# Moving the recurrent unit behind the indexer, and the order of weight chunks that goes with it

## The reference

```python
h = x @ w_in                                    # split among all branches and the gates
# A gated DeltaNet: short causal conv on q, k, v, l2 norm of q and k, chunked rule with a triangular solve
# B sparse attention: rotary, an indexer picks the keys per query (256 of the cache), softmax
# C retention: rotary, multi-scale decay, group norm
# D RG-LRU: conv, then
r  = sigmoid(xb @ w_r + b_r); ig = sigmoid(xb @ w_i + b_i)
a  = exp(-8 * r * softplus(-lam)); b = sqrt(-expm1(2 * log_a)) * (ig * x); h_t = a_t * h_{t-1} + b_t
# E memory cross-attention into 256 memory tokens
ys = each branch * silu(its gate path)
merged = sum(sigmoid(gate_pre[n]) * (ys[n] @ w_branch[n]) for n in range(5))
x = layer_norm(alpha * x + merged @ w_out)
```

## Time and profile before

| | before |
|---|---|
| median of 3 runs | 3231.86 us |
| the profiled execution | 3233.75 us |
| its span, first to last instruction | 3231.9 us |
| PE busy | 2998.8 us, 93% |
| VectorE (DVE) busy | 1702.1 us, 53% |
| ScalarE (ACT) busy | 975.0 us, 30% |
| GpSimd (POOL) busy | 177.1 us, 5% |
| mean granted TensorE clock | 0.947 of full |

### The profile page before, as it was taken

How to read it: one execution, slowest core, us unless ns; L and a number is a source line. 1 busy time by engine, 2 the same in 40 slices (tenths; PEclk the granted TensorE clock), 3 DMA queues, 4 the chain that set the end, 5 groups by cost and what they waited for, 6 DMA issues and landing times. The chain is left out here.

```text
span 3231.9 us, 52427 instructions
## 1 busy us (share of the span) xinstructions
PE 2998.8 (93%) x21612; PEld 2826.4 (87%) x21612; DVE 1702.1 (53%) x2454; ACT 975.0 (30%) x1301; POOL 177.1 (5%) x204
## 2 busy tenths in 40 slices
PE   6998998999999999999789999899999999999995
PEld 5988887998999998999779888789988999989994
DVE  3153367656566756344423533766666657554444
ACT  2232332223253332233313222322233423222232
POOL 0000100000000003100000000000000000030000
PEclk9988998998999999999989889999999999999998
DMA  5565443455656557565256643444655665575661
GB/s 170 163 184 149 144 120 92 115 158 144 175 156 170 148 154 200 166 179 159 70 161 185 194 131 106 127 118 116 168 148 152 168 175 136 161 214 165 167 167 40
DMA packets 830709, 485.98 MB, mean 150 GB/s; under 512 B 26053, under 2 KB 812613, under 8 KB 829219
## 3 DMA queue, kind: packets, MB, share of 16 engines
q1 hardware_dynamic: 809328, 410.00, 47.1%
q0 software_dynamic: 19840, 66.75, 6.6%
q10 hardware_dynamic: 1296, 5.80, 0.5%
HBM read 466.27 MB, written 16.47 MB: 149 GB/s over the span
## 5 line engine op out<-in xcount | busy, mean ns | idle before, releaser
L603 PE MATMUL mb<-xsplit,wsplit 128*128 128x264 f32 (+1 forms) x5312 | 1589.9, 299 | 87.5 <-DVE wsplit L1385 73.8
L604 PE MATMUL mb<-xsplit,wsplit 128*128 128x264 f32 (+1 forms) x5312 | 1538.7, 290 | 0.0
L605 PE MATMUL mb<-xsplit,wsplit 128*128 128x264 f32 (+1 forms) x5312 | 1536.8, 289 | 0.0
L603 PEld LDWEIGHTS mb<-xsplit,wsplit 128*128 128x128 f32 (+1 forms) x5312 | 1031.8, 194 | 124.4 <-issue 54.0
L604 PEld LDWEIGHTS mb<-xsplit,wsplit 128*128 128x128 f32 (+1 forms) x5312 | 1032.2, 194 | 8.0 <-issue 3.8
L605 PEld LDWEIGHTS mb<-xsplit,wsplit 128*128 128x128 f32 (+1 forms) x5312 | 1025.7, 193 | 1.1
L1385 DVE TENSOR_TENSOR wsplit<-ring,wsplit 128x1024 fp32r<-128x1024 f32 (+2 forms) x664 | 776.9, 1210 | 261.3 <-ACT wsplit L1139 247.8
L1139 ACT ACTIVATE wsplit<-ring 128x1024 fp32r<-128x1024 f32 (+2 forms) x664 | 663.3, 1043 | 144.6 <-PE mb L605 104.0
L1166 ACT ACTIVATE gbuf<-mb 128x264 f32<-128x264 f32 x160 | 62.4, 390 | 865.2 <-PE mb L605 852.4
L619 PE MATMUL mb<-work,bring 128*128 128x264 f32 x1280 | 310.6, 385 | 0.0
L1415 DVE TENSOR_TENSOR gbuf<-gbuf,mb 128x264 f32<-128x264 f32 x128 | 54.9, 429 | 456.4 <-PE mb L619 448.8
(11 more groups left out here) (441 smaller groups left out, 2300.6 us busy)
## 6 DMA issues: line engine op xcount, KB each, us to landing
ring<-in_w_in_dram SPq DMA_DIRECT2D x592, 512.0 KB, 4.9
bring<-in_w_branch_dram SPq DMA_DIRECT2D x160, 256.0 KB, 3.1
ring<-in_w_out_dram SPq DMA_DIRECT2D x64, 512.0 KB, 4.5
ring<-in_w_mem_kv_dram SPq DMA_DIRECT2D x32, 512.0 KB, 3.6
work<-in_cache_mem_k_dram POOLq DMA_DIRECT2D x16, 512.0 KB, 4.1
work<-in_cache_mem_v_dram POOLq DMA_DIRECT2D x16, 512.0 KB, 4.2
work<-in_mem_prompt_dram ACTq DMA_DIRECT2D x2, 2048.0 KB, 11.7
work<-in_state_gdn_dram POOLq DMA_DIRECT2D x8, 512.0 KB, 6.6
```

Source lines behind the costliest of these rows:

```text
L603: pe.matmul(bank[0:n, 0:T], wh, ah, start=first, stop=False)
L604: pe.matmul(bank[0:n, 0:T], wh, al, start=False, stop=False)
L605: mm = pe.matmul(bank[0:n, 0:T], wl, ah, start=False, stop=last)
```

## The change

The recurrent unit goes from behind retention to a place directly behind the indexer, on all four engines. Its gate is second in the order of branches (`BRANCH`), and `plan` gives its inputs LX and LZ earlier. The decays, the convolutions, the DeltaNet and retention come behind it, so their steps run beside other chunks: the convolutions beside gate 0, the inverse beside gate 0, RK and gate 1, the DeltaNet's samples beside gate 1, retention beside gate 1, RZ, DK and DV. The norms take 2, 2, 3 and 2 chunks where they took 1, 1, 2 and 3. The unit's results lie in the places of DK, DV and DZ. Its weights are loaded into `tabs` first, by ScalarE at the layer's start as two loads; the levels come after them, by GpSimd, once the second sigmoid is done. Store of RK waits for the unit's last rows, store of RV for the DeltaNet's states, where RZ's store did. 32 chunks are left at the end. In the diff the block of the unit is shown once for each engine where it is added; it is removed unchanged from its old place, apart from indices of waits.

```diff
-PLACE = {GQ: 0, GK: 1, GV: 2, RQ: 3, RK: 4, RV: 5, DQ: 6, DK: 7, DV: 8, DZ: 9, RZ: 10, LZ: 11, IQ: 12, MQ: 13, GZ: 13,
-         MZ: 14, LX: 14}
+PLACE = {GQ: 0, GK: 1, GV: 2, RQ: 3, RK: 4, LX: 4, LZ: 5, DQ: 6, DK: 7, DV: 8, DZ: 9, RZ: 10, RV: 11, IQ: 12, MQ: 13,
+         GZ: 13, MZ: 14}
...
-BRANCH = [(4, MZ), (0, GZ), (2, RZ), (3, LZ), (1, DZ)]
+BRANCH = [(4, MZ), (3, LZ), (0, GZ), (2, RZ), (1, DZ)]
...
-    project(MZ, IQ, DQ, RQ, GQ, GK, GV, GZ, RK, RV)
+    project(MZ, IQ, LX, LZ, RQ, DQ, GQ, GK, GV, GZ)
     gates(0)
-    project(LX, RZ, LZ, DK, DV, DZ)
-    for n in range(1, len(BRANCH)):
-        gates(n)
+    project(RK)
+    gates(1, 0, 12)
+    project(RV)
+    gates(1, 12, KC)
+    project(RZ, DK, DV, DZ)
+    gates(2)
+    gates(3)
+    gates(LAST)
...
-            return H(i_) if i_ < 3 else tmpA
+            return H((DK, DV, DZ)[i_]) if i_ < 3 else tmpA
... PE, behind the indexer
-                    count()
+                    tail(0, LX)
+                    stream(3)
+                    pe.wait_ge(sem.tails_ok, 1)
+                    pe.wait_ge(sem.conv_act, 1)
+                    pe.wait_ge(sem.lw_in, 32)
+                    for i in range(2):
+                        if i:
+                            pe.wait_ge(sem.lru_act, 1)
+                        for h in range(NH):
+                            mm = pe.matmul(bb[:, h, 0:T], lruw[:, i, h, :], H(LX)[:, h, :], start=True, stop=True)
+                        mm.then_inc(sem.lru_mm, 1)
+                        stream(1)
+                    pe.wait_ge(sem.lru_act, 2)
+                    stream(4)
+
+                    pe.wait_ge(sem.lru_o, 1)
+                    for h in range(NH):
+                        mm = pe.transpose(bb[0:NB + 1, 0, h * P:(h + 1) * P], H(LX)[:, h, NP - 1:T], ident)
+                    mm.then_inc(sem.h_mm, 1)
+                    stream(1)
+                    pe.wait_ge(sem.h_rows, 1)
...
                     mm.then_inc(sem.gc_mm, 1)
+                    count()
                     stream(1)
...
-                        stream((1, 1, 2, 3)[n - 1])
+                        stream((2, 2, 3, 2)[n - 1])
...
+                    pe.wait_ge(sem.stored, ready(RV))
... ScalarE
-                                if (x, m) == (RZ, 0):
+                                if (x, m) == (RK, 0):
+                                    act.wait_ge(sem.h_rows, 1)
+                                if (x, m) == (RV, 0):
                                     act.wait_ge(sem.s_out, 16 * NH)
...
-                    act.dma_start(tabs[:, :], a.levels).then_inc(sem.tab_in, 16)
+                    for i, w in enumerate((a.lru_w_r, a.lru_w_i)):
+                        act.dma_start(lruw[:, i, :, :], at_l(w).rearrange("h i j -> i h j")).then_inc(sem.lw_in, 16)
...
+                    stream(1)
+                    ahead()
+                    conv_out(0, LX)
+                    stream(2)
+                    for i in range(2):
+                        ahead()
+                        act.wait_ge(sem.lru_mm, i + 1)
+                        for h in range(CPS):
+                            mm = act.activation(lru(i)[:, h, :], bb[:, h, 0:T], ACT.Sigmoid, bias=qT[:, h, 1 + i:2 + i])
+                        mm.then_inc(sem.lru_act, 1)
+                        stream(1)
+                    for h in range(CPS):
+                        act.activation(lru(2)[:, h, :], lru(0)[:, h, :], ACT.Exp, scale=sn4[:, h:h + 1])
+                        mm = act.activation(lru(3)[:, h, :], lru(0)[:, h, :], ACT.Tanh, scale=sp4[:, h:h + 1])
+                    mm.then_inc(sem.lru_a, 1)
+                    ahead()
+                    stream(1)
+                    ahead()
+                    act.wait_ge(sem.lru_b, 1)
+                    act.activation(lru(0), lru(0), ACT.Sqrt).then_inc(sem.lru_c, 1)
+                    stream(3)
+                    stream(1)
... VectorE
-                            if kind == "gate" and x == LAST and m < 4:
-                                c = slice(4 * m, 4 * m + 4)
+                            if kind == "gate" and x == LAST and 4 <= m < 8:
+                                c = slice(4 * m - 16, 4 * m - 12)
...
+                    conv(0, LX)
+                    stream(2 + 2)
+                    dve.wait_ge(sem.lru_act, 2)
+                    v(dve.tensor_tensor(lru(1), lru(1), H(LX), ALU.mult))
+                    ahead()
+                    dve.wait_ge(sem.lru_a, 1)
+                    ahead()
+                    v(dve.tensor_scalar(lru(0), lru(3), 1.0, None, ALU.add))
+                    v(dve.reciprocal(lru(0), lru(0)))
+                    stream(1)
+                    ahead()
+                    dve.scalar_tensor_tensor(lru(0), lru(3), 2.0, lru(0), ALU.mult, ALU.mult).then_inc(sem.lru_b, 1)
+                    dve.wait_ge(sem.lru_c, 1)
+                    v(dve.tensor_tensor(lru(1), lru(1), lru(0), ALU.mult))
+                    stream(1)
...
                         v(dve.reciprocal(tmpA, tmpA))
                         dve.tensor_tensor(H(s), H(s), tmpA, ALU.mult).then_inc(sem.normed, 1)
-                        stream((1, 1, 2, 3)[n - 1])
+                        stream((2, 2, 3, 2)[n - 1])
...
                     dve.tensor_tensor(H(GZ), H(GZ), H(GQ), ALU.mult).then_inc(sem.normed, 1)
-                    stream(2)
+                    stream(3)
... GpSimd
+                    tail(0, LX)
+                    pool.wait_ge(sem.lru_act, 2)
+                    pool.dma_start(tabs[:, :], a.levels).then_inc(sem.tab_in, 16)
+                    pool.wait_ge(sem.h_rows, 1)
+                    put(o.p_lru[bass.ds(l, 1)].rearrange("z b n -> (z b) n"), stg[0:1, :], sem.lru_out)
+                    put(at_l(o.s_lru), stg[1:NB + 1, :], sem.lru_out)
                     for i, s in enumerate((GQ, GK, GV)):
-                        tail(i, s)
+                        tail(1 + i, s)
```

More of the change, by code:

```diff
@@ L74 @@
 NRING = 4
-BRANCH = [(4, MZ), (0, GZ), (2, RZ), (3, LZ), (1, DZ)]
+BRANCH = [(4, MZ), (3, LZ), (0, GZ), (2, RZ), (1, DZ)]
 LAST = len(BRANCH) - 1
+BRANCH_DONE = [("sy_ok", 1), ("h_rows", 1), ("normed", 3), ("yc_ok", 1), ("sy_ok", 2)]
 def plan():
@@ L87, in project, with gates @@
         chunks.extend(("in", s, m) for s in slots for m in range(CPS))
-    def gates(n):
-        chunks.extend(("gate", n, m) for m in range(KC))
+    def gates(n, m0=0, m1=KC):
+        chunks.extend(("gate", n, m) for m in range(m0, m1))
     project(MQ)
@@ L839, in _, with tail @@
                         pe.wait_ge(sem.sc_ok, j + 1)
-                    count()
+                    def tail(i, s):
+                        pe.wait_ge(sem.stored, ready(s))
+                        if i:
+                            pe.wait_ge(sem.tails_ok, i)
+                        for c in range(CPS):
+                            mm = pe.transpose(bb[0:11, 0, c * P:(c + 1) * P], H(s)[:, c, NP - 3:T], ident)
+                        mm.then_inc(sem.tails, 1)
+                    tail(0, LX)
[4 more added lines that the diff above has]
+                    for i in range(2):
+                        if i:
+                            pe.wait_ge(sem.lru_act, 1)
[11 more added lines that the diff above has]
+                    pe.wait_ge(sem.h_rows, 1)
                     pe.matmul(bb[:, 0, 0:NH], tri_ones[:, 0:P], gbt[:, 0, 0, 0:NH], start=True, stop=True)
@@ L1029, in _ @@
                     pe.wait_ge(sem.yc_ok, 1)
[L1032 to L1054, removed]
                     for n, s in enumerate((DQ, DK)):
@@ L1308, in _ @@
                     roots(4, 1.0 / HD, eps[:, 2:3])
-                    stream(1)
-                    ahead()
-                    conv_out(3, LX)
-                    stream(2)
[L1314 to L1332, removed]
                     stream(2)
@@ L1666, in _ @@
                         stream(1)
[L1668 to L1677, removed]
                     def conv(i, s):
@@ new lines, in _ @@
+                    ahead()
[3 more added lines that the diff above has]
+                    stream(1)
+                    for c in range(CPS):
+                        mm = dve.tensor_tensor_scan(H(LX)[:, c, 0:NP], lru(2)[:, c, 0:NP], lru(1)[:, c, 0:NP], 0.0, ALU.mult, ALU.add)
+                    v(mm)
@@ new lines, in _ @@
+                    ahead()
+                    v(dve.tensor_tensor(H(LX)[:, :, NP:T], lru(2)[:, :, NP:T], qT[:, :, 3:11], ALU.mult))
+                    dve.tensor_tensor(H(LX)[:, :, NP:T], H(LX)[:, :, NP:T], lru(1)[:, :, NP:T], ALU.add).then_inc(sem.lru_o, 1)
+                    stream(2)
+                    dve.wait_ge(sem.lru_o, 1)
+                    dve.wait_ge(sem.stored, ready(LZ))
+                    v(dve.tensor_tensor(H(LZ), H(LZ), H(LX), ALU.mult))
+                    dve.wait_ge(sem.h_mm, 1)
@@ new lines, in _ @@
+                    dve.wait_ge(sem.tail_out, 32)
+                    dve.tensor_copy(stg[0:NB + 1, :], bb[0:NB + 1, 0, :]).then_inc(sem.h_rows, 1)
+                    stream(1)
```

(11 more changed lines are left out.)

62 lines of the change are left out of this document (13 added, 49 removed).

## The result

The changed kernel takes **3235.16 us** (median of 20 runs, 3226.25 to 3239.89); the kernel before, run beside it, 3229.92 (20 runs, 3220.38 to 3234.19). The ratio is **1.0019, interval 1.0010 to 1.0027**: 3 to 9 us slower, 6.1 in the middle. 3229.4 was forecast, 2.4 faster. The change does cost something, and the gain of 7 us a layer that the forecast set against it was real; what was set against that gain was too small.

The account below looks back on a forecast made before the run. TensorE, busy 93% of the span, was taken as the bound, so only its losses could change. Terms summed to -1.2 us a layer, -2.4 over two layers, giving 3229.4 us; range 3216 to 3243, the forecast's own 3225 to 3238.

Parts of the forecast that it names:

- the gain of 7 us a layer: Convolutions of GQ, GK, GV beside gate chunks: loss falls from 8.9 to 2, 0.4 more at the entry; -7.1 us a layer.
- the unit's three: Recurrent unit over short `in` chunks: TensorE waits 1.7 (split behind activations), 4.1 (reciprocal) and 2.7 us (scans).
- the clock's price in the norms: Norms of q and k: 0.7 us each for the lower clock after a 4.3 us wait; changes -1.0 and -1.9 a layer.
- rival 2: Slower: the four long waits (unit, two norms, retention) each pull the clock down, about 1.6 us more each; 3242, chance 0.15.
- the forecast's 2.3: Behind retention: 2.3 us for the falling clock after a 5.5 us wait for `yc_ok`; part of +3.0 a layer.
- The unit's term: Recurrent unit: loss goes from 5.0 us among gates to 8.5 among `in` chunks; +3.5 a layer, from +2.5 to +4.2.
- The forecast's third wait: Recurrent unit: TensorE waits 2.7 us behind the scans, the last of three waits there.
- The inverse: Triangular inverse: a 1.3 us wait goes, two waits grow by 1.4 and 1.8, less 0.4 of merging; +1.5 a layer.
- the DeltaNet's samples: DeltaNet's sample step: four chunks become gates and cover the products' masks; -0.7 us a layer.
- The closed chain: Each convolution with ScalarE's sigmoid and VectorE's merges forms one chain of 17.0 us, against 15.6 us of TensorE's chunks.
- rival 3: Slower: the convolutions' chain binds without the lead (4.5 us more a layer) or with the page's drain (4.1); 3238, chance 0.08.
- the lead: Convolutions: the chain starts some 4 us ahead of TensorE; if absent, the gain is 4.5 us less a layer.

Follow-up runs that it names:

- the run with gates: The changed kernel with gate 0's first four chunks at 46 to 49 beside the recurrent unit, GV's and GZ's moved later: 3229.61 us, ratio 0.9998 against the kernel before.
- The early split: The changed kernel with VectorE's split of the next chunk ahead of its wait for the square root in all four norms: 3197.09 us, ratio 0.9891 against the kernel before.

## Why the prediction was wrong

**The map was right.** All but one of the waits that the forecast named are there, at their places: 3.96 and 4.04 in the middle of the norms (4.3 forecast), 5.23 at the first rotation (5.5), two of the unit's three (1.72 and 3.75 for 1.7 and 4.1), 2.10 ahead of the third chunk, next to none under the convolutions (loss 2.2, forecast 2). No unnamed wait above 0.7 us appeared in these stages. The sum failed by its sizes.

**The failing step is the clock's price in the norms.** The forecast took "about half of 1.5" for the clock after each of the new waits of 4.3 us. With the products in the waits it measured 2.7 and 1.6 a wait, so that the norms gained 0.2 us instead of 2.9. This alone turns the forecast's sum from -1.2 to +1.5 us a layer, from faster to slower. It is the mechanism of rival 2; its price, 0.7 and 1.6 more, is 2.3 a wait, and 2.2 is the mean of what was measured. That rival's 3242 counted the same price at four places; in the unit it cost nothing, as the forecast had argued against it, and behind retention the forecast's 2.3 was already near the measured 2.8 and 2.4. The rows that the forecast had were 1.5 us behind waits of 1.90 and 3.03 and some 3 behind 5.72. A wait of 4.3 lies between them, and so does the measured price; half of 1.5 lay outside both. But no single price would have been right. The waits of 3.96 and 4.04 are the same in both layers and cost 2.7 us each in one and 1.6 in the other. In the kernel before, the unit's wait of 1.90 us has a chunk at a granted clock of 0.78 behind it in layer 1, and the same wait in layer 2 has none:

```profile
2574.47 0.36 PE L603 MATMUL mb<-xsplit,wsplit 128*128 128x264 f32 x1 [1.89 <-DVE wsplit L1385]
2574.50:2582.00 7.50, 7.50 (x56) 7.26 (x57) 4.29 (x7) 1.46 (x3) 0.00 (x0) 1.00 0.93 243
```

The length of a wait doesn't settle what the clock costs behind it; what does isn't shown here.

**The unit's term was 2 us too small.** Before, it lost 5.3 and 3.7 us where the forecast had 5.0: the clock behind its waits cost 2.2 in layer 1 and 0.6 in layer 2, and the rows came from layer 1 alone. After, 9.3 and 10.7 stand against 8.5. The forecast's third wait (2.7) isn't in the changed kernel, whose products run at half clock from 462.4 to 467.6 us, behind the second wait, and fill that time. Where the clock is held by the products that nobody reads, it is there, 2.4 us in both layers (waits of PE in the unit, layer 1):

```profile
PE mb L609 <- DVE wsplit L1413: 3.0, 3, 2.4
```

That the loss comes from the short chunks, the forecast's reason, is shown by the run with gates.

**Errors that offset it.** The convolutions gave 2.2 more than forecast, 1.5 of it ahead of them: the stretch at half clock over the decays' products, in both layers of before, isn't in the new order, and I had left it out. The inverse cost 0.9 less. That 3235 lies inside the forecast's own 3225 to 3238 is in part owed to these two, and so to luck. Against that the DeltaNet's samples and retention lost 1.0 and 0.9 us a layer where -0.7 and 0 stood, without new waits; the clock's falls lie at other places in each run (7.5 and 5.9 in the two layers of one trace, 4.3 and 7.5 with the products), so that I call this scatter, which wasn't tested.

**The closed chain (rival 3) is there, and the lead covers it.** ScalarE's Silu of the three convolutions starts at 507.23, 524.13 and 541.03 us, 16.90 apart; the forecast had 17.0 for the chain and 15.6 for TensorE's chunks. TensorE lost only the wait of 1.77 us at the first square, which fits the lead of some 4 us that the forecast gave it. The table loads in the chain showed no drain: in the changed kernel the Silu ends at 508.32 (507.23 and 1.09), the load starts at 508.33, and the sigmoid starts 1.30 us after the load's start.

```profile
507.23 1.09 ACT L1262 ACTIVATE work<-work 128x1056 f32<-128x1056 f32 x1 [5.93 <-DVE work L1705]
508.33 1.28 ACT L1174 ACT_TABLE_LOAD   x1
509.63 0.39 ACT L1174 ACTIVATE gbuf<-mb 128x264 f32<-128x264 f32 x1
```

The Trainium skill, "ScalarE: Activation LUTs", section "What ACT_TABLE_LOAD costs", has a drain of about 1380 ns beside the load; neither side of this load shows it, and the measurement decides.

**What the forecast didn't ask.** It saw that the second chunk waits for a split behind the reciprocal, and booked the wait; it didn't ask whether the order on VectorE could be another. The early split shows that the change brought the cover and left it unused: 12.7 us a layer of the norms' loss lay in the place of that one call.

## What to carry to other kernels

Work put behind a long step as cover was worth next to nothing here until what it needs itself was issued ahead of that step: a second chunk alone gave 0.2 us a layer, with its split moved into VectorE's idle time 13. Long chunks pay most where the other engines' chains are the bound (four gates were worth 6.6 us beside the unit, 3.9 in the inverse), and moving them is a trade that has to be priced at both places. A forecast in which gains and losses of some 10 us a layer cancel to 1 can't rest on one price for the clock behind a new wait: alike waits of 4.0 us cost 2.7 us in one layer and 1.6 in the other, and the sign of the sum hung on it.

## What the hardware showed

Products that nobody reads, put into TensorE's waits, made the kernel 10 us faster: the granted clock stayed at 1.00 in stretches where it had been 0.88, 0.94 and 0.91. The Trainium skill, "TensorE: Matmul & The Clock Gate", section "The HAM clock gate", says that activity releases a clock that is otherwise throttled; the runs agree, and price it: waits of 4.0 us cost 1.6 to 2.7 us more than themselves. Where the chain of the other engines ended last, in the recurrent unit, the same products gained nothing.
